# Filter and hyena stages: transform at odd half frequencies, even and odd positions apart, inverse over early tiles first

## The reference

```python
def long_conv(u, hf, bias):
    L = u.shape[1]
    U = jnp.fft.rfft(u, n=2 * L, axis=1)
    y = jnp.fft.irfft(U * hf[None], n=2 * L, axis=1)[:, :L]
    return y + u * bias.astype(jnp.float32)

def hyena_mixer(p, n_rows, conv_w, conv_b, filt, bias):
    u = short_conv(p, conv_w, conv_b, n_rows).astype(jnp.float32)
    v, x1, x2 = jnp.split(u, 3, axis=-1)
    hf = hyena_filter_freqs(L, *filt)   # (L+1, 2, C): spectra of two-sided filters
    z = x1 * long_conv(v, hf[:, 0], bias[0])
    y = x2 * long_conv(z, hf[:, 1], bias[1])
    return y.astype(p.dtype)
```

## Time and profile before

| | us |
|---|---|
| median of 3 runs | 4030.69 (4023.37 to 4038.0) |
| the profiled execution | 4025.45 |
| its span, first to last instruction | 4023.3 |
| TensorE matmul busy | 3653.5 (91%) |
| VectorE busy | 2597.4 (65%) |
| ScalarE busy | 1932.2 (48%) |
| GpSimd busy | 800.8 (20%) |

### The profile page before, as it was taken

The page is one execution under the profiler, slowest core; times in us unless marked ns, Lnnn a source line. Parts: engine busy times, 40 slices in busy tenths (PEclk is TensorE's granted clock), DMA queues, the critical chain, the costliest instruction groups (busy, mean ns, idle before and its releaser), DMA issues. The chain is left out here.

```text
span 4023.3 us, 44201 instructions
## 1 busy us (share of the span) xinstructions
PE 3653.5 (91%) x17285; PEld 2886.0 (72%) x17285; DVE 2597.4 (65%) x2867; ACT 1932.2 (48%) x2537; POOL 800.8 (20%) x623
## 2 busy tenths in 40 slices
PE   7999898766788899999999999999998889999988
PEld 4887643466765587888888787778776678787857
DVE  6445356769857888888888887551475625515853
ACT  5211201367562577777677776451365314515731
POOL 2100035400011011111101122320143224203422
PEclk9999899978988999999999999999999899999999
DMA  5553314120055899999999998352521433435123
GB/s 193 206 176 137 117 52 161 59 90 27 29 192 187 306 371 377 373 377 375 366 380 365 380 368 274 131 148 90 178 92 39 153 112 115 133 108 202 52 94 121
DMA packets 322649, 775.03 MB, mean 193 GB/s; under 512 B 26056, under 2 KB 110147, under 8 KB 322184
## 3 DMA queue, kind: packets, MB, share of 16 engines
q1 hardware_dynamic: 299658, 695.40, 47.6%
q0 software_dynamic: 17856, 66.33, 5.1%
q10 hardware_dynamic: 4928, 10.49, 0.7%
HBM read 660.67 MB, written 111.48 MB: 192 GB/s over the span
## 5 line engine op out<-in xcount | busy, mean ns | idle before, releaser
L3225 DVE TENSOR_TENSOR moe_w_low<-shared_z,moe_w_high 128x2048 fp32r<-128x2048 f32 x256 | 590.2, 2351 | 101.5 <-ACT moe_w_high L3178 101.4
L3178 ACT ACTIVATE moe_w_high<-shared_z 128x2048 fp32r<-128x2048 f32 x256 | 476.6, 1917 | 169.0 <-DMA shared_z<-in_exp_w 161.8
L177 PE MATMUL moe_bank<-moe_w_high,moe_xgT_high 128*128 128x512 f32 x1024 | 402.4, 393 | 4.9 <-POOL moe_xgT_low L3067 4.9
L178 PE MATMUL moe_bank<-moe_w_low,moe_xgT_high 128*128 128x512 f32 x1024 | 400.1, 391 | 0.0
L179 PE MATMUL moe_bank<-moe_w_high,moe_xgT_low 128*128 128x512 f32 x1024 | 400.1, 391 | 0.0
L3225 DVE TENSOR_TENSOR moe_w_low<-moe_w_raw,moe_w_high 128x2048 fp32r<-128x2048 f32 x128 | 287.3, 2286 | 60.2 <-ACT moe_w_high L3178 60.0
L3178 ACT ACTIVATE moe_w_high<-moe_w_raw 128x2048 fp32r<-128x2048 f32 x128 | 238.4, 1912 | 105.2 <-DMA moe_w_raw<-in_exp_w 96.2
L3453 POOL TENSOR_SCALAR layer_att_p<-layer_att_p,layer_att_rinv,layer_att_neg_lam 128x1280 f32<-128x1280 f32 (+1 forms) x72 | 173.4, 2408 | 523.8 <-DVE layer_att_neg_lam L3482 309.4
L3460 DVE TENSOR_REDUCE layer_att_nb<-layer_att_scores 128x1 f32<-128x1280 f32 (+1 forms) x144 | 194.9, 1369 | 85.2 <-PE layer_att_scores L3365 84.3
L177 PE MATMUL layer_front_bank<-layer_front_w_high,layer_front_hT_high 128*128 128x512 f32 (+1 forms) x608 | 229.6, 378 | 7.4 <-POOL layer_front_hT_low L800 7.4
L177 PEld LDWEIGHTS moe_bank<-moe_w_high,moe_xgT_high 128*128 128x128 f32 x1024 | 193.6, 189 | 45.8 <-POOL moe_xgT_low L3067 6.0
(11 more groups left out here) (604 smaller groups left out, 8575.7 us busy)
## 6 DMA issues: line engine op xcount, KB each, us to landing
shared_z<-in_exp_w SPq DMA_DIRECT2D x128, 2048.0 KB, 10.0
moe_w_raw<-in_exp_w SPq DMA_DIRECT2D x64, 2048.0 KB, 10.1
shared_z<-in_w_in SPq DMA_DIRECT2D x48, 512.0 KB, 6.6
first_raw<-in_w_in SPq DMA_DIRECT2D x32, 512.0 KB, 7.5
front_vec<-in_ada_w POOLq DMA_DIRECT2D x16, 1024.0 KB, 6.0
late_raw<-in_w_mod SPq DMA_DIRECT2D x8, 2048.0 KB, 8.0
...
```

The costliest lines, as they stand in the source:

```text
L177: nc.tensor.matmul(out, lhs[0], rhs[0], start=start, stop=False)
L178: nc.tensor.matmul(out, lhs[0], rhs[1], start=False, stop=False)
L3178: nc.scalar.activation(hi, x, ACT.Copy).then_inc(high, 1)
L3225: nc.vector.tensor_tensor(lo, x, hi.bitcast(F32), ALU.subtract).then_inc(low, 1)
```

## The change

The spectra are taken at odd half frequencies, (2k + 1)/2 in place of k. None of them is its own mirror, so no frequency needs a row of its own: the `lag0` matmuls of the filter, the `cols` matmuls, the `rest` rows and the six one-row operations go. The tables of the forward and the inverse hold cos + sin for the folded sums and cos - sin for the differences. The middle position still needs one row, in all four cosine units (L1842 of the new kernel), and the inverse an edge of one column at each quarter (L1856 of the new kernel). Further:

- The odd half of a forward unit is computed first, and the copy of it starts when it is done (`odd_done`).
- In quarters 0 to 2 the subtraction for q moves from VectorE to GpSimd; in quarter 3 VectorE does it and the last pair of q.
- In the inverse tiles 0, 1 and 3 do their first half for quarters 0 to 2 as the quarters come; banks are assigned anew (`ring`, `turning`).
- Convolutions 6 and 7 get their side terms during the products; 9 stands behind the results of order one, 10 and 11 inside the first quarter of order two. The last fold of order two is VectorE's.
- The loads for the next stage wait for the last forward unit. The squares are summed after the last tile. Root and reciprocal are in the output stage.
- GpSimd waits for the stores of the filter before it sets `ones`, and the first transposes no longer wait for `ones`.

```diff
-                                                    fold[o][s][:, jj, :], start=(j == 0), stop=(j == HF - 1 and not (f == 0 and s == 1 and odd == 0)))
-                        if f == 0 and s == 1 and odd == 0:
-                            for j in range(HF):
-                                last = nc.tensor.matmul(bank[4 + 2 * (i % 2)][:, :], lag0[:, 2:2 + P], fold[o][0][:, j, :],
-                                                        start=False, stop=(j == HF - 1))
...
+        ring, turning = [(2, 4, 6), (2, 4, 0)], (0, 6)
...
-                sp.wait_ge(q_ready, 2 * FT)
-                sp.wait_ge(middle, 2)
+                sp.wait_ge(spectrum, 2 * UN)
...
+                core.stored(pool, core.hstore[0:6])
...
+                        nc.gpsimd.tensor_tensor(G[1][:, a, :], G[1][:, a, :], t[2][:, :], ALU.subtract).then_inc(q_summed, 1)
...
+                SIDES = {(0, 1): [(6, 0)], (0, 2): [(6, 1)], (0, 3): [(6, 2)], (0, 4): [(7, 0)], (0, 5): [(7, 1)], (0, 6): [(7, 2)],
+                         (1, 0): [(11, 0)], (1, 1): [(11, 1)], (1, 2): [(11, 2)]}
...
+                        copy_result(0)
+                        side_terms(8)
+                        copy_result(1)
+                        side_terms(9)
+                        copy_result(2)
+                        place_u(CH)
+                        copy_result(3)
+                        place_u(CH + 1)
+                        place_u(CH + 2)
+                        side_terms(10)
+                        place_u(CH + 3)
                     else:
...
+                        copy_result(CH)
+                        head_forward_logs(act)
+                        copy_result(CH + 1)
+                        square(0)
+                        head_backward_logs(act)
+                        copy_result(CH + 2)
+                        square(1)
+                        copy_result(CH + 3)
+                        square(2)
+                        square(3)
+                        head_carried(act)
...
+                    for half, to in ((1, odd), (0, even)):
+                        more = half == 0 and s == 0
                         for k in range(2):
                             j = 2 * half + k
-                            more = half == 0 and (f == 0 or f == 1 and s == 0)
-                            last = nc.tensor.matmul(to[:, w], fwd[s][:, j, f * P:(f + 1) * P], src[:, j, w],
+                            last = nc.tensor.matmul(to[:, w], fwd[s][:, j, f * P:(f + 1) * P], u[s][:, j, w],
                                                     start=(k == 0), stop=(k == 1 and not more))
...
-                        if half == 0 and s == 1 and f == 0:
-                            for j in range(2):
-                                nc.tensor.matmul(to[:, w], cols[:, 0:P], u[0][:, j, w], start=False, stop=False)
-                            nc.tensor.matmul(to[:, w], cols[0:1, 0:P], u[1][0:1, 0, w], start=False, stop=True)
...
+                def edge(n, f):
 
                     o, c = divmod(n, CH)
+                    nc.tensor.matmul(result(n)[1][:, 0:1], G[0][:, slots(o, f)[2], c * P:(c + 1) * P], ones[:, 0:1],
+                                     start=False, stop=False)
+
+                def first_half(n, f):
+                    o = n // CH
+                    pe.wait_ge(p_paired, FT * o + f + 1)
+                    back_term(n, f, 0, 0)
+                    if f < FT - 1:
+                        pe.wait_ge(q_paired, (FT - 1) * o + f + 1)
                     else:
+                        pe.wait_ge(q_last, o + 1)
+                        edge(n, f)
+                    back_term(n, f, 1, 0)
+                    if f < FT - 1:
+                        edge(n, f)
+
+                def second_half(n):
+                    for r in range(2):
                         for f in range(FT):
+                            last = back_term(n, f, r, 1)
                     last.then_inc(back, 1)
+
+                def inverse(o):
+                    for c in (0, 1, 3):
+                        pe.wait_ge(u_ready if c == 3 else released, 2 * CH * (o + 1) if c == 3 else UN * o + 6 + c)
+                        for f in range(FT - 1):
+                            first_half(CH * o + c, f)
+                    for c in range(CH):
+                        n = CH * o + c
+                        if c == 2:
+                            pe.wait_ge(released, UN * o + 8)
+                            for f in range(FT - 1):
+                                first_half(n, f)
+                        first_half(n, FT - 1)
+                        second_half(n)
+                        if o == 0 and c == 2:
...
-                        if o and c:
-                            square_sums(c - 1)
-                last = square_sums(CH - 1)
...
-                    if f == 0:
-                        step(last)
-                        r0, r1 = t[0][0:1, :], t[1][0:1, :]
-                        step(nc.vector.tensor_tensor(rest[0][:, :], r0, r1, ALU.subtract))
-                        nc.vector.tensor_tensor(rest[1][:, :], q[0:1, :], d1_[0:1, :], ALU.mult)
-                        step(nc.vector.tensor_tensor(r0, q1[0:1, :], d_[0:1, :], ALU.mult))
-                        step(nc.vector.scalar_tensor_tensor(rest[1][:, :], rest[1][:, :], -1.0, r0, ALU.mult, ALU.subtract))
-                        nc.vector.memset(r0, 0.0)
-                        last = nc.vector.memset(r1, 0.0)
-                    last.then_inc(p_ready, 1)
-                    nc.vector.tensor_tensor(q, q, c_, ALU.mult)
-                    step(nc.vector.tensor_tensor(q1, q1, c1_, ALU.mult))
-                    nc.vector.tensor_tensor(G[1][:, a, :], q, t[2][:, :], ALU.add)
-                    step(nc.vector.tensor_tensor(G[1][:, b, :], q1, t[3][:, :], ALU.add))
+                    nc.vector.tensor_tensor(t[0][:, :], v_, d_, ALU.mult)
+                    nc.vector.tensor_tensor(t[1][:, :], u1_, d1_, ALU.mult).then_inc(p_ready, 1)
+                    last = f == FT - 1
+                    nc.vector.tensor_tensor(v_ if last else G[1][:, a, :], v_, c_, ALU.mult)
+                    step(nc.vector.tensor_tensor(u1_, u1_, c1_, ALU.mult))
+                    if last:
+                        nc.vector.tensor_tensor(v_, v_, t[2][:, :], ALU.subtract)
+                    step(nc.vector.tensor_tensor(G[1][:, b, :], u1_, t[3][:, :], ALU.add))
+                    dve.sem_inc(q_ready, 1)
+                    if last:
+                        dve.wait_ge(q_paired, (FT - 1) * (o + 1))
+                        nc.vector.tensor_tensor(G[1][:, e, :], v_, G[1][:, b, :], ALU.add)
+                        step(nc.vector.tensor_tensor(G[1][:, b, :], v_, G[1][:, b, :], ALU.subtract))
+                        dve.sem_inc(q_last, 1)
                     dve.sem_inc(released, 1)
-                    dve.sem_inc(q_ready, 1)
 
...
+                def last_fold():
+                    n = 2 * CH - 1
+                    half, tile = SEQ // 2, mix[CH - 1]
+                    add, sub = fs[n % 2]
+                    dve.wait_ge(turned, 2 * (n - 1))
+                    nc.vector.tensor_copy(add[:, 0:1], tile[:, half:half + 1])
+                    nc.vector.tensor_copy(sub[:, 0:1], tile[:, 0:1])
+                    nc.vector.tensor_tensor(add[:, 1:half], tile[:, 1:half], tile[:, half + 1:SEQ], ALU.add)
+                    nc.vector.tensor_tensor(sub[:, 1:half], tile[:, 1:half], tile[:, half + 1:SEQ], ALU.subtract
+                                            ).then_inc(last_folded, 1)
...
+                for f in range(FT):
+                    sum_products(0, f)
+                    difference_products(0, f)
+                conv_with_sides(6)
+                finish(0)
+                conv_with_sides(7)
+                finish(1)
+                conv_with_sides(8)
+                finish(2)
+                finish(3)
+                last_fold()
+                conv_with_sides(9)
+                for f in range(FT):
+                    sum_products(1, f)
+                    if f == 0:
+                        conv_with_sides(10)
+                    difference_products(1, f)
+                    if f == 0:
+                        conv_with_sides(11)
+                head_keys()
+                finish(CH)
+                head_sums(0)
+                finish(CH + 1)
+                finish(CH + 2)
+                finish(CH + 3)
+                head_sums(1)
                 dve.wait_ge(ssq, 1)
-                nc.vector.tensor_reduce(core.hy_rms[:, :], bank[0][:, 0:NT * CH].rearrange("p (c t) -> p t c", t=NT), AX, ALU.add
-                                        ).then_inc(ssq_summed, 1)
-                dve.wait_ge(rooted, 1)
-                step(nc.vector.reciprocal(core.hy_rstd[:, :], core.hy_rms[:, :]))
+                nc.vector.tensor_reduce(core.hy_rms[:, :], bank[0][:, 0:NT * CH].rearrange("p (c t) -> p t c", t=NT), AX, ALU.add)
         for j in range(RAW):
```

(8 more changed lines are left out.)

295 lines of the change are left out of this document (112 added, 183 removed).

## The result

The changed kernel takes 3981.69 us, median of four runs (3977.88 to 3987.24); the one before, measured again beside it, 4028.88 us (4023.37 to 4038.0). The ratio is 0.9882, with a 95% interval of 0.9858 to 0.9905: 47.2 us less. The forecast was 3988, range 3973 to 4008. The profiled execution took 3984.71 us. Both kernels were measured once more later: 3977.48 against 4031.83 us, 54 us less (experiment 10).

A forecast was written before the change was run, and what follows sets the result against it. Different engines lead each stretch; products, last sums, inverse and hand-over stand one behind the other, twice. Terms -6.3, -18.2, -18.8, +0.4 sum to -42.9 us, giving 3982.6 profiled; the median lies 5.2 above, so 3988, range 3973 to 4008.

The forecast's parts named there:

- the 3982.6 of the sum: Whole kernel: the profiled execution's 4025.45 us less the summed gain of 42.9 us.
- Filter, -6.3: Filter on TensorE: two blocks of four matmuls go, giving 3.43 and 2.85 us; bounds -3.4 and -6.9.
- Start of hyena to first part, 0: Stretch before VectorE's first part: input comes by DMA at 356 GB/s, so no change; bounds -1 and +1.5.
- Products: VectorE's quarters in order one: 8.79 us each, the first down from 15.35, the fourth 10.7; GpSimd gets seven sums.
- The 1.96 us stall: VectorE's wait for TensorE's second unit goes: three matmuls fewer (2.8 us), odd half copied without waiting for the even.
- the 0.6 us per subtraction: Products, quarters one to three: moving one subtraction to GpSimd shortens VectorE's quarter from 9.39 to 8.79 us.
- Inverse of order one: TensorE does tiles 0, 1 and 3 partly early; order two's first part at 745.2 against 763.45: -18.2 us.
- Order two, -18.8: Order two: hidden sums, early tiles, no square sums between tiles, tail 1.4 us longer; bounds -8 and -23.
- Rival A: TensorE's clock stays low until tile 0 is done, 10 us more, twice: gain 23, 4008 us; chance 0.12.
- B: Slower: low clock through the whole inverse, 116 matmuls at 0.6 us more, 4054 us; chance 0.03.
- C: Tiles wait for banks or side terms hold copies, so inverses begin as late as before: gain 19, 4012; chance 0.06.
- D: More gain: no shared-port cost, all 6.9 in the filter, no low clock: gain 54, 3977 us; chance 0.08.

The follow-up runs named there:

- experiment 10: The changed kernel itself, unedited, measured again beside the kernel before: 3977.48 us against 4031.83; hyena stage 179.25 us.
- experiment 5: Changed kernel with the filter's two blocks of four matmuls put back as weight alone: hyena starts at 644.44 us, against 638.9 in the changed kernel.
- experiment 3: Changed kernel with six one-row operations put back in each order's first quarter, as weight alone: hyena stage 188.5 us, against 179.2.
- experiment 6: Changed kernel with two full-width matmuls and a one-row one put back in each order's second forward unit, as weight alone: hyena stage 179.5 us, against 179.2.
- experiment 11: Changed kernel, but each forward unit computes its even half first, as before: hyena stage 181.7 us, against 179.2.
- experiment 2: Changed kernel with the q subtraction of quarters one to three back on VectorE: hyena stage 176.5 us, against 179.2.
- experiment 8: Changed kernel with three 512-column matmuls, as weight alone, in TensorE's wait for each order's third q pair: hyena stage 175.1 us, against 179.2.
- experiment 12: Changed kernel, but gate projections are loaded when VectorE has done its last products, as before: hyena stage 180.0 us, against 179.2; order two stays at 81.6.
- experiment 1: Changed kernel, but tiles 1 and 3 do their first halves behind the last quarter of products, only tile 0 early: hyena stage 189.3 us, against 179.2.
- experiment 4: Changed kernel, but early first halves go by quarters: one and two of tiles 0, 3, 1, then each third quarter: hyena stage 172.8 us, against 179.2.

## Why the prediction was right

The mechanism was right in its main lines and the sum was 5.1 us short at the end of hyena; the median came to 6 us from the forecast, and to 10.5 in the second measurement. That the profiled execution, 3984.71 us, lies 2 us from the 3982.6 of the sum is luck: the 5.1 us too few and 7.6 us of scatter in the later stages nearly cancel.

- Filter, -6.3: the start of hyena moved by -7.2, but that mixes three things. The row from which experiment 5 counts the filter comes 1.4 us later (476.80 against 475.43). From there the filter is 8.6 us shorter, of which about 2 are a clock step that comes and goes from one execution to the next. The two blocks are worth 6.0 to 6.7 us with the clock alike, so the term was right. The 0.9 us beyond it are scatter, not the edit.
- Start of hyena to first part, 0: measured -0.4, less than its scatter (19.7 to 22.4 us).
- Products: VectorE done at 37.2 us (37.1 said) and 43.3 (43.9), GpSimd's third q pair at 34.0 (34.2) and 39.9 (40.6). The removal of one-row operations held to 0.1 us (experiment 3). Two reasons did not hold. The 1.96 us stall went because the second unit comes earlier, not because it lost three matmuls (experiment 6) or because its odd half comes first (experiment 11). And the 0.6 us per subtraction moved to GpSimd were no gain: GpSimd's chain sets when TensorE goes on, and the third q pair comes 0.6 us later for it. The orders were 2.5 to 3.6 us longer with it, nearly all in order one, where the clock differed too (experiment 2).
- Inverse of order one: early tiles done at 43.6 us (43.2 said), tiles at 48.2, 52.8, 60.6, 66.1 (47.8, 52.4, 60.3, 65.8), order two at 76.8 (78.0). I had charged 1.6 to 1.8 us an order for the low clock; by the blocks it cost 2.4 and 1.7 in this profile, and 1.7 to 3.2 over all (experiment 8). ScalarE held result 2, as said, until 720.7, but for 0.4 us only. The 1.2 us lie behind tile 3: the copies of the last turn (733.52) waited for TensorE and not behind side terms, so they were done 0.8 us sooner than I had them.
- Order two, -18.8: measured -21.3. Early tiles and tiles came about 1 us before their forecast; the tail was too long by 1.4 us: I had summed scan, what follows it and the exponentials as 8.6 us, and they took 7.2 (810.54 to 817.76). Of the edits I had named for this part, the earlier loads gave nothing (experiment 12).
- That early tiles pay was right: 9 to 10 us in both orders together (experiment 1).

Taken back one at a time, the edits account for about half of the 48.4 us: 6.0 to 6.7 for the filter's blocks, 7.6 to 8.7 for the one-row operations, 9.2 to 10.3 for early tiles 1 and 3, 1.2 to 1.8 for one group of square sums. The other edits, above all the convolutions that moved out of the inverses, the last q pair on VectorE and the new tail, were not taken back by themselves, so for the other half the cause is argued from positions and not shown.

Rival A is the one with truth in it: the clock does eat into the early tiles, 3.8 to 4.9 us in both orders (experiment 8), of which 3.2 to 3.6 were in my sum already. A had 20 on top of those. Its condition (low until tile 0 is done) did not occur after; in experiment 1, with a longer wait, tile 0 did run low. B and C are out: eight records behind the first block take 1.89 us, the third q pair comes at 34.0, and ScalarE's copies wait behind side terms for 0.4 us at most. (In order two a copy waits 1.1 us behind the logarithms, at 795.65.) D asked for no low clock, and it was low in both orders. The Trainium skill (TensorE: Matmul & The Clock Gate, Loop structure matters more than you think) has the clock fall where a long wait stands before every matmul. Here one wait per block was enough, as the window at 0.77 shows.

One thing kept the gain smaller than it could be: the order of the early tiles. Two quarters each of tiles 1 and 3, whose inputs are long there, stand behind tile 0's wait for its third q pair. By quarters the orders are 6.8 to 7.9 us shorter (experiment 4).
